# Modulated rows handed to TensorE in quarters of 256 features instead of halves of 512

## The reference

```python
for l in range(DEPTH):
    mod = (sc @ w_ada[l] + b_ada[l]).reshape(B, N_SUBLAYERS, 3, D_MODEL)[:, :, :, None, :]
    m = mod[:, 0]
    y = _swiglu(_modulate(x, m), ffn_w_up[l, 0], ffn_w_down[l, 0])
    x = _layer_norm(DEEPNORM_ALPHA * x + 0.5 * (1.0 + m[:, 2]) * y, ln_g[l, 0], ln_b[l, 0])
    ... # the mixer with m = mod[:, 1], then the second FFN with m = mod[:, 2]
def _modulate(x, m):
    return x * (1.0 + m[:, 1]) + m[:, 0]
```

## Time and profile before

| what | value |
|---|---|
| median of three timed runs | 1382.29 us |
| span of the profiled execution (its only own time; nothing lies around it in the profile) | 1384.3 us |
| TensorE matmuls (PE) | 1320.7 us busy, 95% |
| VectorE (DVE) | 971.7 us, 70% |
| ScalarE (ACT) | 660.3 us, 48% |
| mean granted TensorE clock | 0.971 |

### The profile page before, as it was taken

How to read it: one execution, slowest core, us unless ns; L and a number is a source line. 1 busy time by engine, 2 the same in 40 slices (tenths; PEclk the granted TensorE clock), 3 DMA queues, 4 the chain that set the end, 5 groups by cost and what they waited for, 6 DMA issues and landing times.

```text
span 1384.3 us, 18624 instructions
## 1 busy us (share of the span) xinstructions
PE 1320.7 (95%) x7396; PEld 1102.5 (80%) x7396; DVE 971.7 (70%) x1227; ACT 660.3 (48%) x974; POOL 127.1 (9%) x218
## 2 busy tenths in 40 slices
PE   2899999999999999999999999989999999999996
PEld 2688888798888777888878888879978878788885
DVE  6577765597776767888467877468787667676555
ACT  0544443667744436444344444256775353544431
POOL 6000001000000010001100000100000001100000
PEclk7899999999999999999999999999999999999999
DMA  9688873866555447888549888457656542785550
GB/s 354 213 277 280 278 268 86 272 214 201 169 193 183 139 132 244 281 278 279 200 139 303 275 277 292 144 162 255 216 184 194 184 150 86 245 285 187 191 192 31
DMA packets 194086, 295.24 MB, mean 213 GB/s; under 512 B 14248, under 2 KB 158160, under 8 KB 194000
## 3 DMA queue, kind: packets, MB, share of 16 engines
q1 hardware_dynamic: 173488, 220.57, 47.6%
q0 software_dynamic: 20512, 73.48, 17.6%
HBM read 292.97 MB, written 1.05 MB: 212 GB/s over the span
## 4 chain that ended last, share of the span: by engine, by line
PE 82%; DVE 7%; ACT 4%; issue 2%; DMA 2%; SPq 2%; POOL 1%; POOLq 0%; ACTq 0%; DVEq 0%
PE pg L927 71%; PE pt L952 1%; DVE wlo L1504 1%; PE pt L887 1%; ACT lnw L512 1%; DMA wraw<-in_w_in_dram 1%; SPq L257 1%; DMA wraw<-in_ffn_w_up_dram 1%; ACT whi L530 1%; PE pt L1255 1%; PE pt L1242 1%; PE pt L896 1%; DVE cv L1671 1%; PE pt L1257 1%; SPq L265 1%
## 5 line engine op out<-in xcount | busy, mean ns | idle before, releaser
L1504 DVE TENSOR_TENSOR wlo<-wraw,whi 128x1024 fp32r<-128x1024 f32 (+1 forms) x408 | 480.0, 1202 | 185.3 <-ACT whi L530 185.0
L530 ACT ACTIVATE whi<-wraw 128x1024 fp32r<-128x1024 f32 (+1 forms) x408 | 405.9, 1035 | 223.3 <-PE pg L927 130.9
L927 PE MATMUL pg<-whi,hhi 128*128 128x512 f32 x1024 | 416.2, 406 | 10.4 <-DVE hlo L1492 9.6
L927 PE MATMUL pg<-whi,hlo 128*128 128x512 f32 x1024 | 404.9, 395 | 0.0
L927 PE MATMUL pg<-wlo,hhi 128*128 128x512 f32 x1024 | 404.9, 395 | 0.0
L927 PEld LDWEIGHTS pg<-whi,hhi 128*128 128x128 f32 x1024 | 196.3, 192 | 53.7 <-DVE hlo L1492 11.8
L927 PEld LDWEIGHTS pg<-whi,hlo 128*128 128x128 f32 x1024 | 195.7, 191 | 42.6
L927 PEld LDWEIGHTS pg<-wlo,hhi 128*128 128x128 f32 x1024 | 196.2, 192 | 39.3 <-issue 1.0
L1528 DVE SCALAR_TENSOR_TENSOR acc<-aw,sc,acc 128x1024 f32<-128x1024 f32 x128 | 163.8, 1279 | 0.0
L927 PE MATMUL pg<-whi,athi 128*128 128x512 f32 x352 | 141.0, 401 | 0.0
L927 PE MATMUL pg<-whi,atlo 128*128 128x512 f32 x352 | 139.2, 396 | 0.0
(11 more groups left out here) (322 smaller groups left out, 1333.5 us busy)
## 6 DMA issues: line engine op xcount, KB each, us to landing
wraw<-in_ffn_w_up_dram SPq DMA_DIRECT2D x176, 512.0 KB, 5.7
aw<-in_w_ada_dram POOLq DMA_DIRECT2D x128, 512.0 KB, 4.6
wraw<-in_w_in_dram SPq DMA_DIRECT2D x104, 512.0 KB, 5.1
wraw<-in_ffn_w_down_dram SPq DMA_DIRECT2D x88, 512.0 KB, 4.6
pro<-in_w_ada_dram SPq DMA_DIRECT2D x8, 1024.0 KB, 14.0
wraw<-in_w_branch_dram SPq DMA_DIRECT2D x16, 512.0 KB, 4.3
wraw<-in_w_o_dram SPq DMA_DIRECT2D x16, 512.0 KB, 4.1
lnw<-in_ln_g_dram POOLq DMA_DIRECT2D x5, 512.0 KB, 4.1
```

What stands on the lines that cost most here:

```text
L530: act.activation(hi_view(n)[:, 0:size], wraw[:, q, o:o + size], ACT.Copy).then_inc(S["w_hi"], 1)
L927: ins = pe.matmul(out_ap, a[i], b[j], start=first and n == 0, stop=last and n == 2, skip_group_check=group)
L1504: dve.tensor_tensor(lo, a, hi_view(n)[:, 0:size].bitcast(F32), ALU.subtract).then_inc(S["w_lo"], 1)
```

## The change

A half of 512 features becomes two quarters of 256 in three places. ScalarE's `modulate` does two scalings, the wait for its own, and one rounding of 128 x 256, and this twice. VectorE's `h_low` does two subtractions of 128 x 256, each with its own wait. TensorE waits at step q for quarter q. The semaphores `h_f32`, `h_hi` and `h_lo` count twice as far. The order of the calls on each engine, the scalings' number, the matmuls, the transposes and the loads stay as they are.

```diff
-    "x_gain": 6, "o_rs": 2, "h_f32": 12, "h_hi": 12, ...
+    "x_gain": 6, "o_rs": 2, "h_f32": 24, "h_hi": 24, ...
-    "h_lo": 12, "w_lo": 204, "ln_gy": 12, "ln_sum": 12,
+    "h_lo": 24, "w_lo": 204, "ln_gy": 12, "ln_sum": 12,
-    "mod_cols": 1, "h_f32": 4, "h_hi": 4, "h_lo": 4,
+    "mod_cols": 1, "h_f32": 8, "h_hi": 8, "h_lo": 8,
...
-                        pool.wait_ge(S["h_lo"], 4 * (stage + 1))
+                        pool.wait_ge(S["h_lo"], 8 * (stage + 1))
...
             def modulate(at, k, t, half):
 
-                n = 2 * (NT * k + t) + half + 1
                 act.wait_ge(S["mod_cols"], at("mod_cols", k + 1))
-                act.wait_ge(S["ln_xt"], at("ln_xt", n))
-                for c in range(4 * half, 4 * half + 4):
-                    ins = act.activation(lnw[:, t, c * P:(c + 1) * P], pt[:, 2 * t + half, (c % 4) * P:(c % 4 + 1) * P],
-                                         ACT.Identity, bias=modab[:, 1, c:c + 1], scale=modab[:, 0, c:c + 1])
-                ins.then_inc(S["h_f32"], 1)
-                act.wait_ge(S["h_f32"], at("h_f32", n))
-                act.activation(hhi[:, 4 * half:4 * half + 4, t * P:(t + 1) * P],
-                               lnw[:, t, half * 512:(half + 1) * 512].rearrange("p (k s) -> p k s", k=4),
-                               ACT.Copy).then_inc(S["h_hi"], 1)
+                act.wait_ge(S["ln_xt"], at("ln_xt", 2 * (NT * k + t) + half + 1))
+                for quarter in (2 * half, 2 * half + 1):
+                    n = 4 * (NT * k + t) + quarter + 1
+                    for c in (2 * quarter, 2 * quarter + 1):
+                        ins = act.activation(lnw[:, t, c * P:(c + 1) * P], pt[:, 2 * t + half, (c % 4) * P:(c % 4 + 1) * P],
+                                             ACT.Identity, bias=modab[:, 1, c:c + 1], scale=modab[:, 0, c:c + 1])
+                    ins.then_inc(S["h_f32"], 1)
+                    act.wait_ge(S["h_f32"], at("h_f32", n))
+                    act.activation(hhi[:, 2 * quarter:2 * quarter + 2, t * P:(t + 1) * P],
+                                   lnw[:, t, quarter * 256:(quarter + 1) * 256].rearrange("p (k s) -> p k s", k=2),
+                                   ACT.Copy).then_inc(S["h_hi"], 1)
...
-                            pe.wait_ge(S["h_lo"], at("h_lo", 2 * (NT * (s - 1) + t) + q // 2 + 1))
+                            pe.wait_ge(S["h_lo"], at("h_lo", 4 * (NT * (s - 1) + t) + q + 1))
...
-                            pe.wait_ge(S["h_lo"], at("h_lo", 2 * t + q // 2 + 1))
+                            pe.wait_ge(S["h_lo"], at("h_lo", 4 * t + q + 1))
...
             def h_low(at, k, t, half):
 
-                c = slice(4 * half, 4 * half + 4)
-                dve.wait_ge(S["h_hi"], at("h_hi", 2 * (NT * k + t) + half + 1))
-                dve.tensor_tensor(hlo[:, c, t * P:(t + 1) * P],
-                                  lnw[:, t, half * 512:(half + 1) * 512].rearrange("p (k s) -> p k s", k=4),
-                                  hhi[:, c, t * P:(t + 1) * P].bitcast(F32), ALU.subtract).then_inc(S["h_lo"], 1)
+                for quarter in (2 * half, 2 * half + 1):
+                    c = slice(2 * quarter, 2 * quarter + 2)
+                    dve.wait_ge(S["h_hi"], at("h_hi", 4 * (NT * k + t) + quarter + 1))
+                    dve.tensor_tensor(hlo[:, c, t * P:(t + 1) * P],
+                                      lnw[:, t, quarter * 256:(quarter + 1) * 256].rearrange("p (k s) -> p k s", k=2),
+                                      hhi[:, c, t * P:(t + 1) * P].bitcast(F32), ALU.subtract).then_inc(S["h_lo"], 1)
```

More of the change, by code:

```diff
@@ L31 @@
     "prm_in": 64, "ln_rows": 96, "ln_rstd": 6, "ln_var": 6,
-    "x_gain": 6, "o_rs": 2, "h_f32": 12, "h_hi": 12, "w_hi": 204, "up_silu": 44, "act_hi": 22, "mix_ev": 14, "sm_T": 1, "sm_in": 1,
+    "x_gain": 6, "o_rs": 2, "h_f32": 24, "h_hi": 24, "w_hi": 204, "up_silu": 44, "act_hi": 22, "mix_ev": 14, "sm_T": 1, "sm_in": 1,
     "conv0": 3, "conv": 9, "conv_silu": 3, "cv_sq": 2, "sp_exp": 1, "ea": 1, "beta_e": 1, "sp_ln": 1, "nrm_ln": 1,
```

## The result

The changed kernel takes 1377.17 us, the median of five runs (1374.85 to 1378.09), against 1382.29 of five runs of before (1380.67 to 1386.39). The ratio is 0.995, 95% interval 0.9934 to 0.9967: 6.9 us faster, 4.6 to 9.1; the two medians by themselves lie 5.1 apart. A later repeat, beside runs of before on its own chip, gave 0.9953 (0.9936 to 0.997). The forecast was a gain of 3.7 us: right in sign, too small against both intervals.

What follows compares the result with a forecast made beforehand. TensorE was taken as the bound, holding 82% of the chain, so only its stalls could be won. Entries -4.78 and start +1.06 gave -3.7 us: 1378.6 from a median of 1382.3, own range 1377.3 to 1380, wide range 1376 to 1382.8.

Steps and rivals of the forecast that it cites:

- The first quarter, 1.19 us earlier: At entries for t = 1: TensorE goes on at T (first scaling) + 1.76 instead of T + 2.95.
- Later quarters keep up, and weight half 4 just holds: At t = 1 quarters come every 1.17 us against TensorE's 1.37; in FFNs weight half 4 keeps 0.4 us of slack.
- t = 0 costs 0.07 to 0.10 per entry: VectorE's chain into T, the first scaling of t = 1, moves later by 0.10 behind an FFN, 0.07 behind the mixer.
- Start +1.06: At the kernel's start, ScalarE's row work ahead of weight half 3 lasts 1.06 us longer, going through to the end.
- The fallen clock: Rival, chance 0.20: the clock falls at the kernel's start, costing 1.5 us, upper bound 2.5; time 1380.1 to 1381.1.
- The fifth entry, 0.39: At the last entry (T = 1189.39), where TensorE ran at the lower clock, the gain is only 0.39 us.
- The mixer's DMA "can only help": In the mixer, gain rows' loads now come just behind the weight unit's DMA, which can only help; no size in the sum.
- a rival with 0.10: More than forecast, chance 0.10: TensorE's mixer wait on the unit's DMA goes too, 0.5 each: 1377.6, or clock luck.
- the part on counts: GpSimd's wait comes some 0.4 later, gain rows are first read over 20 us later; no DMA moves past another queue.

Runs made afterwards that it cites:

- e6: Against the kernel before: halves at the start and for t = 0; for t = 1 two quarters, then one half of 512. Ratio 0.9977, -3.2 us.
- e7: Against the kernel before: halves at the start and for t = 0; for t = 1 eight single blocks of 128. Ratio 0.9996, -0.6 us.
- e5: Against the kernel before: the whole change, with weight half 3 split between t = 0 and t = 1 at the start. Ratio 0.9933, -9.3 us.
- e8: Kernel before, halves everywhere, with GpSimd's gain and shift row loads at the two mixer entries held until weight half 3 is used. Ratio 0.9995.

## Why the prediction was right and wrong

- *The first quarter, 1.19 us earlier*: right. T + 1.76 in the trace, 1.18 at entries 1 to 4. Rounding 0.42, subtraction 0.42 and the period 1.17 were 0.418, 0.422 and 1.16. The slope over three copy sizes was good enough.
- *Later quarters keep up, and weight half 4 just holds*: right. No wait came with quarters; e6 and e7, one step coarser and one finer, each show a wait close to the one computed ahead of the run.
- *t = 0 costs 0.07 to 0.10 per entry*: too dear; 0.04.
- *Start +1.06*: right in size (+1.09, with 0.17 to 0.21 of it from before the rows). The idle ahead of q = 3 was 2.70 in the repeat, as the forecast's 2.6 had it. In the change's own profile it was 4.15: there the clock rose at 44 instead of 47.6 and q = 2 ended at 47.0 instead of 48.4. *The fallen clock*, a rival with 0.20, happened in each of three profiles and cost 1.4 to 1.6, as priced. It should have been part of the likeliest case.
- *The fifth entry, 0.39*: with the next one the step that failed most. It took one execution's low clock for a feature of the place. In the other profiles with quarters this entry gave 1.63 (1.00 in e5, where the clock fell nearby); of this about 0.45 is clock alone, since e8 has it without quarters.
- *The mixer's DMA "can only help"*: the mechanism was right, but the sum has it at nothing, and the size (0.5 each) stood in a rival with 0.10; the part on counts even says that no DMA is moved past another queue, which this order of two loads is. It is 1.38 us in five of nine profiles (0.69 in the change's first profile).
- *With the measured terms the forecast comes to about -5.1*: -5.9 at the entries, -0.45 clock at the fifth, -1.38 at the DMA, +0.2 for t = 0, +0.9 and +1.5 at the start. It lies inside both measured intervals (4.6 to 9.1 and 4.2 to 8.9); -3.7 lies outside. That -3.7 came as near as it did is luck: a gain of 2.6 us was missing in it (1.24 at the fifth entry, 1.38 at the DMA) and a loss of 1.5 (the clock at the start). With the 0.69 of the change's first profile in place of 1.38 the sum is -4.4.
- What the timed runs show beyond 5.1, 1.4 to 1.8 us, is not settled. It is one low stretch of the clock more or less and within the interval, but all seven columns with quarters for all of t = 1 have an excess of the same sign, so chance alone is not shown either.
- The median of before that the forecast started from was low: later sets of runs gave 1385.01 (17 runs), 1383.42 (29) and 1385.97 (11).

## What to carry to other kernels

Cut a hand-over finer only until the first piece arrives when its user is free, and keep the period of the pieces under the user's time for one: here 1.16 us against 1.37. Pieces of one block brought the period to 1.39 and made the following weights late by 0.62; one whole half behind the first two quarters was too coarse and gave back 0.73 to 0.79. Ask what stands behind the lengthened instruction on its engine at every place where the code is used; at the one place where it loses, splitting the next weights ahead of part of the row work turned a loss of 2.6 us into a gain of 2.2 by the starts of matmuls. Price no stretch from one execution when the clock was low in it: read the same matmuls in two traces and look at the steps.

## What the runs showed of the hardware

Low stretches of the granted clock that differ by 3.4 us between two traces move everything behind them by 1.6 us. They come where TensorE does thin work, such as 32 matmuls of one column in 4.08 us at 1160.81, and not inside the long runs of 512 columns. The idles differ in what they do: of 26 idles of 2.45 to 2.52 us (two entries in each of thirteen traces) the clock fell in six, or within 1.5 us behind them; of the three at the start, 2.70, 3.65 and 4.15 us long and soon after the clock's rise, it fell at all three. ScalarE's wait for its own last instruction is cheap: in e7 the rounding starts 0.03 us behind the end of the scaling that it waits for (718.92 + 0.44 to 719.39).
